# A two-part transformer kernel: the second part's first norm becomes a head inside the projection stage, and the context's keys and values move into the first part

## The reference

```
for l in 0, 1:                                   # first part
    x = x + 0.5 * swiglu(rms_norm(x), ffn1)
    proj = rms_norm(x) @ w_in[l]                 # 256 x 5120
    o_a = rwkv7_mixer(proj, ...)                 # scan
    o_b = diff_attention(proj, ...)
    x = x + (sum of gated o_a @ w_branch0, o_b @ w_branch1) @ w_out[l]
    x = x + 0.5 * swiglu(rms_norm(x), ffn2)

for l in 0, 1:                                   # second part
    m = silu(c) @ mod_w[l] + mod_b[l]            # 6 x 1024: sh1 sc1 g1 sh2 sc2 g2
    h = rms_norm(x, norm1_g[l]) * (1 + sc1) + sh1
    if l == 0:
        mc = silu(c_ctx) @ mod_w[0] + mod_b[0]
        hc = rms_norm(ctx, norm1_g[0]) * (1 + csc1) + csh1
        pr = h @ attn_in_w                       # 256 x 1792: q, k, v, u, v
        ctx_kv = hc @ attn_in_w[:, 512:768]      # keys and values of the context
        y = window attention over [pr.kv, ctx_kv] beside a gated unit, @ attn_out_w
    else:
        y = multiscale_pool(h)
    x = x + g1 * y
    h2 = rms_norm(x, norm2_g[l]) * (1 + sc2) + sh2
    x = x + g2 * peer_ffn(h2)                    # 8 x 16 gathered experts for each token
out = rms_norm(x, final_g)
```

## Time and profile before

| | us |
|---|---|
| median of 3 runs | 3282.35 |
| lowest, highest | 3281.87, 3284.14 |
| the profiled execution, its time | 3290.93 |
| its span in the trace | 3288.7 |
| from the last feed-forward matmul of the first part to the last matmul of the projection | 1697.99 to 1815.98 |

### The profile page before, as it was taken

How to read it: one execution, slowest core, us unless ns; L and a number is a source line. 1 busy time by engine, 2 the same in 40 slices (tenths; PEclk the granted TensorE clock), 3 DMA queues, 4 the chain that set the end, 5 groups by cost and what they waited for, 6 DMA issues and landing times. The chain is left out here.

```text
span 3288.7 us, 45326 instructions
## 1 busy us (share of the span) xinstructions
PE 2873.9 (87%) x16786; PEld 1918.8 (58%) x16786; DVE 2142.2 (65%) x3990; ACT 1310.8 (40%) x2973; POOL 575.4 (17%) x516
## 2 busy tenths in 40 slices
PE   7999988899999998879988999997778789777777
PEld 5877787678787778757856765432322555233222
DVE  5755665577575576566744577777775577777774
ACT  4433432344443353054423434444443334444443
POOL 0000000000000000000000024444444034444442
PEclk9999999899999999999997999999999999999999
DMA  7745201377585530126754269999999699999997
GB/s 267 266 170 169 86 3 41 128 257 276 184 281 186 178 111 3 41 80 241 262 218 162 84 261 427 427 427 426 427 427 427 234 391 426 427 427 427 427 427 313
DMA packets 252571, 858.38 MB, mean 261 GB/s; under 512 B 15031, under 2 KB 138807, under 8 KB 179517
## 3 DMA queue, kind: packets, MB, share of 16 engines
q0 software_dynamic: 73728, 536.90, 38.8%
q1 hardware_dynamic: 178622, 318.59, 27.7%
HBM read 847.05 MB, written 8.39 MB: 260 GB/s over the span
## 5 line engine op out<-in xcount | busy, mean ns | idle before, releaser
L3206 POOL DMA_INDIRECT raw_weights<-peer_rows,expert_ids x208 | 232.8, 1119 | 2281.2 <-DVE expert_ids L148 1993.5
L447 PE MATMUL banks<-weight_parts_hi,normedT_hi 128*128 128x512 f32 (+2 forms) x1152 | 459.3, 399 | 38.0 <-DVE weight_parts_lo L1147 12.0
L3316 PE MATMUL banks<-raw_weights,diagonals 128*128 128x512 f32 x832 | 404.8, 630 | 85.2 <-ACT diagonals L181 85.0
L449 PE MATMUL banks<-weight_parts_hi,normedT_lo 128*128 128x512 f32 (+2 forms) x1152 | 448.5, 389 | 0.0
L448 PE MATMUL banks<-weight_parts_lo,normedT_hi 128*128 128x512 f32 (+2 forms) x1152 | 448.0, 389 | 0.0
L3316 PE MATMUL banks<-query_weights,diagonals 128*128 128x512 f32 x704 | 336.2, 618 | 61.2 <-ACT diagonals L181 61.1
L3316 PEld LDWEIGHTS banks<-raw_weights,diagonals 128*128 128x128 f32 x832 | 156.9, 198 | 325.1 <-ACT diagonals L181 171.9
L157 DVE CUSTOM_DVE_ANT_0 modulation<-raw_weights,normed 128x1024 f32<-128x1024 f32 x208 | 255.1, 1226 | 139.6 <-DMA raw_weights<-peer_rows,expert_ids 129.0
L3316 PE MATMUL banks<-modulation,diagonals 128*128 128x512 f32 x512 | 246.7, 619 | 58.9 <-ACT diagonals L181 58.8
L181 ACT ACTIVATE gelu<-dots 128x1 f32<-128x1 f32 x512 | 101.9, 199 | 477.5 <-DVE dots L157 476.8
L157 DVE CUSTOM_DVE_ANT_0 modulation<-query_weights,normed 128x1024 f32<-128x1024 f32 x176 | 215.7, 1226 | 112.3 <-DMA query_weights<-peer_rows,expert_ids 102.7
(11 more groups left out here) (402 smaller groups left out, 4940.1 us busy)
## 6 DMA issues: line engine op xcount, KB each, us to landing
raw_weights<-ffn_in SPq DMA_DIRECT2D x88, 1024.0 KB, 7.6
side_weights<-mod_tiles SPq DMA_DIRECT2D x48, 1024.0 KB, 5.3
raw_weights<-ffn_out SPq DMA_DIRECT2D x44, 1024.0 KB, 5.9
raw_weights<-w_in SPq DMA_DIRECT2D x28, 1024.0 KB, 5.0
query_weights<-peer_w_q SPq DMA_DIRECT2D x16, 1024.0 KB, 10.9
raw_weights<-w_in SPq DMA_DIRECT2D x10, 1536.0 KB, 6.5
raw_weights<-w_branch SPq DMA_DIRECT2D x8, 1024.0 KB, 6.9
raw_weights<-w_out SPq DMA_DIRECT2D x8, 1024.0 KB, 6.2
```

The source lines that it names most:

```text
L447: nc.tensor.matmul(out, lhs.hi, rhs.hi, start=start, stop=False)
L449: return nc.tensor.matmul(out, lhs.lo, rhs.hi, start=False, stop=stop)
L3206: nc.gpsimd.indirect_dma_start(out=ring.rows(g), out_offset=None, in_=table, in_offset=bass.IndirectOffsetOnAxis(ap=ids[:, n, t:t + 1], ax ...
L3316: last = nc.tensor.matmul(k.bank(2 * j + half), diag[:, g % DIAGS, :], ring.rows(g)[:, D + half * BANK:D + (half + 1) * BANK], start=t == ...
```

## The change

Three edits hang together.

- **Side sums begin from the biases.** A new input holds each bias block as a [128 x 512] tile whose first row is the bias and the rest zero. `SideSums.bias` loads it into the accumulator before the first unit of a pair is added; in `step` this load first waits for the store that used the accumulator last. `make` waits for it, and its first operation is a multiply-add as the others. All bias matmuls and bias rows of the second part go. The order of the blocks changes a little.
- **The context's keys and values** (`ContextKV`) are made in layer 1 of the first part. `linear_stage` of w_in loads the context and squares it on ACT at its end; `QkNorm` takes the root along; `finish_mixers` loads the side sums needed, the context transposed and the weights (seven DMAs, 4 MB, into the upper half of `raw_weights` and a new buffer), sums them over the partitions into columns with 32 matmuls of two columns each (in place of `keep_warm(k, 0, 8)`), builds shift @ W and scales the transposed context by its gain column; `turn_split_stage` ends with the other half of the product and two operations of DVE. These products are plain f32 matmuls. The result goes to DRAM in the w_out stage and is read back in the projection stage.
- **The second part's first norm** is a `ShiftedHead` of the projection's `linear_stage`. ACT copies with scale and bias, and DVE makes the whole value in one operation, waits with a drain, and subtracts in another. The projection's first two weight tiles are loaded at the end of the last feed-forward stage (`w_first[2]` is now `w_pr`, with `start=1`). `modulations`, `norm_pair_stage` and the context's `linear_stage` go. What they loaded and is still needed (7 DMAs of side sums of 5 MB, five tables, the context's keys and values) is now `extra`, issued by SP at the start of the projection stage. The eight row sums move to `window_mix`, where they take the place of its first and second `keep_warm`.

```diff
-def turn_split_stage(k, jobs):
+def turn_split_stage(k, jobs, beside=None):
...
+            if beside is not None:
+                beside.pe_products(pe, 1)
...
+            if beside is not None:
+                beside.dve_finish(dve, Ops(nc, dve, True))
...
     def step(self, sp, i):
         if i >= len(self.which):
             return
         sp.wait_ge(self.k.sem["side_done"], i + 1)
         self.load(sp, i + 2)
+        if i >= 2 and i % 2 == 0:
+            self.bias(sp, i + 2)
...
+    def bias(self, sp, i):
+
+        if i >= len(self.which):
+            return
+        n, u = self.which[i] // 2, i // 2 % 2
+        if i >= 4:
+            sp.wait_ge(self.k.sem[f"side_out{u}"], self.stores(i - 4))
+        for who in range(2 if n in self.both else 1):
+            sp.dma_start(self.acc[:, u, who], self.biases[n]).then_inc(self.k.sem[f"part_in{u}"], 16)
...
-                if n % 2 == 0 and kc_ == 0:
-                    last = o.ts(acc, w, c, ALU.mult, free=True)
-                else:
-                    last = o.stt(acc, w, c, acc, ALU.mult, ALU.add, free=True)
+                last = o.stt(acc, w, c, acc, ALU.mult, ALU.add, free=True)
...
+class ShiftedHead(NormHead):
...
+    def act_copies(self, act, o, j, n):
+        act.wait_ge(self.k.sem["turned"], j * KC // 2 + n + 1)
+        for c, bank, hi, _ in self.chunks(j, n):
+            last = o.fn(hi, bank, ACT.Identity, scale=self.gain(c), bias=self.shift(c), free=True)
+        last.then_inc(self.k.sem["copied_s"], 1)
+
+    def dve_lows(self, dve, o, j, n):
+        dve.wait_ge(self.k.sem["copied_s"], j * KC // 2 + n + 1)
+        whole = lambda c: self.k.junk[:, c % 4 * P:(c % 4 + 1) * P]
+        for c, bank, _, _ in self.chunks(j, n):
+            o.ts(whole(c), bank, self.gain(c), ALU.mult, self.shift(c), ALU.add, free=True)
+        dve.drain()
+        for c, _, hi, lo in self.chunks(j, n):
+            last = o.sub(lo, whole(c), hi.bitcast(F32), free=True)
+        last.then_inc(self.k.sem["copied_v"], 1)
...
         for last, n in early:
             if last < 0:
                 ahead.load(k, sp, n, n % 2)
+        for dst, src in extra:
+            sp.dma_start(dst, src).then_inc(k.sem["written"], 16)
...
+    def pe_columns(self, pe):
+        k, C = self.k, self.k.const
+        pe.wait_ge(k.sem["part_in0"], self.loaded)
+        for who in range(2):
+            for c in range(2 * KC):
+                at = 2 * (who * 2 * KC + c)
+                last = k.nc.tensor.matmul(k.bank(2)[:, at:at + 2], self.sums[:, who, c * P:(c + 1) * P], C("ones"),
+                                          start=True, stop=True)
+        last.then_inc(k.sem["rows_made"], 1)
+
+    def pe_shift(self, pe):
+        k = self.k
+        pe.wait_ge(k.sem["shifted"], 1)
+        for c in range(KC):
+            last = k.nc.tensor.matmul(k.bank(6)[:, 0:2 * KVW], self.wide[:, c, :], self.w[:, c, :], start=c == 0, stop=c == KC - 1)
+
+    def pe_products(self, pe, j):
+        k = self.k
+        for c in range(KC):
+            last = k.nc.tensor.matmul(k.bank(4 + j)[:, 0:2 * KVW], self.xT[:, c, j * P:(j + 1) * P], self.w[:, c, :],
+                                      start=c == 0, stop=c == KC - 1)
+        if j == 1:
+            last.then_inc(k.sem["summed"], 1)
+
+    def dve_columns(self, dve, o):
+        k = self.k
+        dve.wait_ge(k.sem["rows_made"], 1)
+        made = k.bank(2)[:, 0:8 * KC].rearrange("p (c two) -> p c two", two=2)[:, :, 0]
+        folded = k.folded[:, :, :, :].rearrange("p w s c -> p (w s c)")
+        o.copy(folded, made, free=True)
+        gain = k.gains[:, DEPTH * 3 * KC:(DEPTH * 3 + 1) * KC]
+        for who in range(2):
+            o.stt(k.folded[:, who, 1, :], k.folded[:, who, 1, :], 1.0, gain, ALU.add, ALU.mult, free=who > 0)
+        o.copy(self.wide, spread(k.folded[:, 0, 0, :], P), free=True).then_inc(k.sem["shifted"], 1)
+
+    def dve_scale(self, o):
+        k = self.k
+        o.mul(self.xT, self.xT, spread(k.folded[:, 0, 1, :], SEQ)).then_inc(k.sem["grown"], 1)
...
+    def dve_finish(self, dve, o):
+        k = self.k
+        dve.wait_ge(k.sem["used"], 1)
+        dve.wait_ge(k.sem["summed"], 1)
+        for j in range(NT):
+            o.stt(self.kv[:, j, :], k.bank(4 + j)[:, 0:2 * KVW], self.root[:, j:j + 1], self.shift, ALU.mult, ALU.add, free=True)
...
-                keep_warm(k, 0, 8)
+                if context is None:
+                    keep_warm(k, 0, 8)
+                else:
+                    context.pe_columns(pe)
+                    context.pe_shift(pe)
+                    pe.wait_ge(S["grown"], 1)
+                    pe.wait_ge(S["stored"], N - 1)
+                    context.pe_products(pe, 0)
...
+                if context is not None:
+                    context.dve_columns(dve, o)
                 for j in range(NT):
                     dve.wait_ge(S["y_normed"], j + 1)
                     o.mul(y[:, j, :], y[:, j, :], gained[:, j, :], free=True)
                     if j == 0:
                         o.add(y[:, j, :], y[:, j, :], rest[:, j, :])
+                        if context is not None:
+                            context.dve_scale(o)
...
+        xn = mod[:, 0:2 * D].rearrange("p (j d) -> p j d", j=NT)
         linear_stage(k, lambda c_, j: hT[:, c_, j * P:j * P + P], w_pr, IN_W // 4,
-                     lambda o, t, j, bank: o.copy(pr[:, j, bass.ds(t * (IN_W // 4), IN_W // 4)], bank, free=True), w_mix)
-        window_mix(k, room, pr, kvc, mod[:, 0:2 * D].rearrange("p (j d) -> p j d", j=NT))
+                     lambda o, t, j, bank: o.copy(pr[:, j, bass.ds(t * (IN_W // 4), IN_W // 4)], bank, free=True), w_mix,
+                     head=ShiftedHead(k, k.folded[:, 1], hT, xn, rs), extra=extra)
+        window_mix(k, room, pr, kvc, mod[:, 0:2 * D].rearrange("p (j d) -> p j d", j=NT), ones, RowSums(k, mod, ones))
```

More of the change, by code:

```diff
@@ L723, in square_pieces, with stream @@
             act.wait_ge(changed, b + 1)
-        o.fn(k.junk[:, :], k.X[:, b // 2, b % 2 * BANK:(b % 2 + 1) * BANK], ACT.Square,
+        o.fn(k.junk[:, :], x[:, b // 2, b % 2 * BANK:(b % 2 + 1) * BANK], ACT.Square,
              total=k.squares[:, b // 2, b % 2:b % 2 + 1])
-def stream(k, block, wts, ahead, size, parts, done, done_per, finish_steps, act_steps=None, side=None, head=None, act_end=None):
+def stream(k, block, wts, ahead, size, parts, done, done_per, finish_steps, act_steps=None, side=None, head=None, act_end=None,
+           extra=()):
     nc = k.nc
@@ L777, in _ @@
             side.end(sp)
+        if extra:
+            sp.wait_ge(k.sem["written"], 16 * len(extra))
     @block.scalar
@@ L867, in slot, with linear_stage @@
     return parts[:, u, :].rearrange(f"p ({names}) -> p {names}", **dims)
-def linear_stage(k, lhs, wts, width, finish, ahead=None, groups=NT, head=None):
+def linear_stage(k, lhs, wts, width, finish, ahead=None, groups=NT, head=None, extra=(), act_end=None):
     nc = k.nc
@@ L904, in finish_steps, with linear_sum_stage @@
                 finish(o, t, j, k.bank(u * groups + j)[:, 0:width]).then_inc(drained, 1)
-        stream(k, block, wts, ahead, size, parts, summed, groups, finish_steps, head=head)
+        stream(k, block, wts, ahead, size, parts, summed, groups, finish_steps, head=head, extra=extra, act_end=act_end)
     k.clear()
-def linear_sum_stage(k, lhsT, kc, wts, finish, ahead=None, side=None, squares=False):
+def linear_sum_stage(k, lhsT, kc, wts, finish, ahead=None, side=None, squares=False, extra=()):
     nc = k.nc
@@ L988, in _ @@
                 side.load(sp, 0)
+                side.bias(sp, 0)
+                side.bias(sp, 2)
                 sp.wait_ge(S["turned"], KC)
@@ L1454, in prepare, with rwkv @@
         k.clear()
-def rwkv(k, gain, w_proj, w_rest, proj, mu, w0, w2, a0, a2, g2, k_k, k_a, r_k, row_loads, columns, out, out_b, lamc, lam_now, ahead):
+def rwkv(k, gain, w_proj, w_rest, proj, mu, w0, w2, a0, a2, g2, k_k, k_a, r_k, row_loads, columns, out, out_b, lamc, lam_now, ahead,
+         context=None):
     nc = k.nc
@@ L1556, in act_squares @@
         act.wait_ge(S["reduced"], 1)
+        if self.other is not None:
+            o.fn(self.other[:, :, 0], self.other[:, :, 0], ACT.Sqrt, free=True)
         o.fn(self.ss[:, :, :], self.ss[:, :, :], ACT.Sqrt, free=True).then_inc(S["rooted"], 1)
@@ L1880, in rwkv_tiles, with finish_mixers @@
         k.clear()
-def finish_mixers(k, proj, y, qT, move, fresh, gained, rest, lam, gain_col, sub_gain, out, ahead):
+def finish_mixers(k, proj, y, qT, move, fresh, gained, rest, lam, gain_col, sub_gain, out, ahead, context):
     nc = k.nc
@@ L2276, with sum_runs, __init__ @@
+def sum_runs(l, first, last):
+    where = {lb: (half, n) for half, blocks in enumerate(SideSums.BLOCKS) for n, lb in enumerate(blocks)}
+    out = []
+    for blk in range(first, last):
+        half, n = where[l, blk]
+        if out and out[-1][1] == half and out[-1][2] + out[-1][3] == n:
+            out[-1][3] += 1
+        else:
```

(7 more changed lines are left out.)

320 lines of the change are left out of this document (121 added, 199 removed).

## The result

Eighteen runs of each kernel: the changed one takes 3262.15 us in the median, the one before 3283.93. The ratio is 0.9932, with a 95% interval of 0.9922 to 0.9942: 22 us faster, where 55.9 were forecast.

A forecast was written before the change was run, and what follows sets the result against it. The prediction took the second part's front to be a string of waits, with no engine as bound. Its terms, -64.0 + 6.9 + 2.5 - 2.0 + 0.7 = -55.9 us, took 3282.35 to 3226 us, range 3217 to 3239.

The forecast's parts named there:

- no term: Peers' gathers: twelve bias matmuls go, but the DMA engines are full, so nothing is gained; no term for a changed length.
- the gathers' window unchanged at 427 GB/s: Sign of being right: in the peers' gathers the DMA rate stays at 427 GB/s.
- The columns, +6.9: Layer 1's finish_mixers: 64 narrow records at about 0.107 us and DVE's work delay branch_a's second product by 6.9 us, bounds 5 and 9.
- the clock falls in the mixers' end: Rival: narrow records and waits for DVE bring TensorE to half clock at the mixers' end, costing 12 us, 3238; chance 0.12.
- 2.5 was said: turn_split_stage: transposes, the product's second half and two DVE operations take 7.3 us instead of 4.8, +2.5 us.
- The first branch matmuls, -2.0: Stage after turn_split_stage: with one idle stretch filled its start no longer runs at half clock, -2.0 us, other bound 0.
- The front, -64.0: Last feed-forward matmul to last of the projection: 54.0 us instead of 118.0, tile 1 starting at 25.0; 64.0 us saved.
- Tile 2 in time, cost 0: Projection: tile 2's load lands between 22 and 25 us, needed by 27.4, cost 0; rival of it late, 14 us, chance 0.10.
- a sign of being wrong: Projection: ACT waiting for attn_in_w in tile 2 would show the forecast wrong.
- Biases, cost 0: Feed-forward stages: 28 added loads, multiply-adds and 16 store waits cost 0, with 7.8 us of cover for each wait.
- slower, by the bias waits: Rival: SP's 16 store waits hold up feed-forward tiles, 3.5 us each taking the whole gain, 3291 at 19 us; chance 0.02.

The follow-up runs named there:

- Experiments 1 to 5: Unused arrays of 32 to 160 bytes ahead of raw_weights: two on the changed kernel, ratios 0.9932 and 0.9876; three on the kernel before, 1.0059 to 1.0068.
- e1_pad96: The changed kernel with an unused array of 96 bytes a partition ahead of raw_weights: 3249.94 us, ratio 0.9876 to the kernel before.
- experiment 8: e1_pad96 with 128 columns of ones instead of 2 in the 64 passes, issued in four pieces within the last attention rounds: 3230.13 us, ratio 0.9831.
- e1_pad32: The changed kernel with an unused array of 32 bytes a partition ahead of raw_weights: 3268.11 us, ratio 0.9932 to the kernel before.
- e1_columns_in_loop: e1_pad32 with the 64 two-column passes issued in four pieces within the second mixer's last attention rounds: 3263.14 us, ratio 0.9918.
- e3_tile1_early: experiment 8 with tile 1's cast and low part made before the second half of tile 0 in the projection's head: 3233.86 us, ratio 0.9823.

## Why the prediction was wrong

The forecast was 3226 us in a range of 3217 to 3239; it took 3262. Four terms of the sum were off.

- **The gathers, "no term": the largest miss.** The step that failed is "the gathers' window unchanged at 427 GB/s": the prediction looked at the matmuls that go and at the DMA engines being full, and put the stretch at nothing. The change added 160 bytes ahead of the gathers' targets in SBUF, and they moved 421 GB/s. Experiments 1 to 5 price that at 18 to 22 us; it is more than half of the 33.6 us that are missing. The edit has nothing to do with norms, contexts or biases: e1_pad96 is the same change, 41 us faster than before.
- **The columns, +6.9: right mechanism, half clock not counted.** The 64 passes were priced at 0.107 us from a row of eight at full clock and took 0.171, 10.97 in all; the rival "the clock falls in the mixers' end" happened, and I had given it 0.12, which was too little. My argument against it put two rows together that don't belong together: eight narrow records at 1304.55 and a pause among 512-wide matmuls at 1450.65 say nothing of 64 narrow records in a run. `finish_mixers` became 12.9 us longer instead of 6.9. The shift's product took 5.89 instead of 4.0. DVE's part was 0.9 less than forecast: its broadcast copy of 1024 elements took 0.68, not 1.1, about half of the 1.23 of the two-operand row, and 0.2 was a slip (1427.6 + 0.6 + 1.1 is 1429.3). `turn_split_stage` cost +1.9 where 2.5 was said. The whole was +14.8 instead of +9.4; by experiment 8, 13.7 us of it can be had back.
- **The first branch matmuls, -2.0:** -0.6 came. Their first 4.8 us ran at 0.64 of the clock, where before it was 0.52: behind a pause of 2.67 us the clock was not at 1.00, as a row with 2.45 us had let me expect.
- **The front, -64.0:** it gave -59.3, since the way to the projection's end took 58.7 us instead of 54.0. Two terms were too small. `ShiftedHead`'s added operations took 0.69 us a pair and not 0.47, 0.8 us over the four pairs; and the bias operand of ACT's copy, for which I had charged nothing, made its eight copies 2.91 us instead of 2.17, 0.7 us on the way to tile 1. With these, and 0.2 more at the first half's last pair, tile 1 starts 26.7 us after the feed-forward, as it did in the later runs, instead of 25.0. In this profiled execution the first fall of the clock (1723.3 to 1729.4) still lasted when PE did the last pair of tile 0's first half, which added 0.8: 27.5. From tile 1 on it was 2.1 more: 1.4 by the second fall of the clock, where 8 passes started in 3.0 us instead of some 15, and 0.7 because a pass takes 0.205 us at full clock and not 0.2.
- **Tile 2 in time, cost 0:** right. ACT did wait for `attn_in_w`, which I had named as a sign of being wrong, by 2.06 us (timeline of the changed kernel), but PE was at tile 1 until about 1751 and the cast was done at 1741.5; the wait cost nothing.

```profile
1738.33 3.18 ACT L840 CAST weight_parts_hi<-raw_weights 128x3584 fp32r<-128x3584 f32 x1 [2.06 <-DMA raw_weights<-attn_in_w]
```

- **Biases, cost 0:** right. Layer 1's second feed-forward stage took 201.8 us before and after (1498.0 to 1699.8, 1512.7 to 1714.5). The rival "slower, by the bias waits" has a slip in its last figure: with stores of 19 us each wait would be 19 - 13.4 = 5.6 us, 90 for the sixteen, so 34 slower and not 9; nothing hangs on it.
- **What stays open.** -55.9 with 18 for the gathers, 5.4 for the mixers' end, 4.7 for the front and 1.4 for the branches is -26, and -22.3 was measured, with an interval of 3 us to either side. The mixers' end was not the same in each execution (65.8 us in the profiled run, 68.1 in those of e1_pad32 and e1_pad96, with the same code), which would be 2 of the 4; and with the upper price of the gathers, 22, the sum is -22. I have not measured more of it.

## What to carry to other kernels

Before any "unchanged" stage is priced at zero, ask what the edit does to the addresses of the buffers that its DMAs fill: where a stage is bound by DMA, keep its targets at multiples of 256 bytes of a partition, and check them after each small array is added. Filler matmuls that are replaced with useful narrow ones are not an even trade: price what follows at either clock, and make the operand wide or spread the passes between wide ones. When a copy gets an added operation or operand, price it on each engine that the next tile waits for: here DVE's cost the first half of a tile, ACT's bias the second. And when a reordering seems to have cured a low clock, look at the whole stage: the pause may only have moved.

## What the runs showed of the hardware

- DMA into SBUF at full queues: 427 GB/s with targets at a multiple of 256 bytes, 419 to 421 at remainders of 32, 128, 160 and 192, for rows of 8192 bytes; 536.9 MB so take 18 to 24 us more. Other arrays moved along with the targets.
- Passes of 128 x 2 in an unbroken run had the granted clock at 0.50 with PE 13.70 of 13.70 us busy (e1_pad96); in e1_columns_in_loop, among the attention's products, it fell from 1.00 to 0.63 while PE was busy for 9.20 of 9.20 us; with passes of 128 x 128 on the same weights in the same place it was 1.00. Sixteen of the wide ones took 1.95 us there, sixteen narrow ones 1.84 at full clock and 3.41 at half.
- A pause of PE of 2.57 us ahead of tile 1 had 3 us at 0.59 behind it; in e3_tile1_early a pause of 2.63 us lay ahead of tile 0's second half, with 3.3 us at 0.51 behind it, and tile 1, without a pause, ran at 1.00.
- ACT's copies of 128 x 128 out of PSUM: eight took 2.91 us with scale and bias, 2.17 to 2.18 with scale alone. DVE's f32 copy of 1024 elements between SBUF buffers took 0.68 us.
